# A streaming encoder step on one core: head sums of queries in two one-pass products, and eight attention units behind the gate units of the last projection tile

## The chip, the cores and the metric

The kernel runs on one core of a Trainium2 chip. The metric is the device time of one execution in microseconds. The kernel before takes 1554.57 us, the median of 3 runs (1553.36 to 1554.69). The engines in the profile are PE (TensorE, matrix products), DVE (VectorE), ACT (ScalarE), POOL (GpSimd) and SP (SyncE, which issues most DMAs).

## The reference

The model has two layers with 1024 channels over a prompt of 2048 frames and a sample of 64 frames, all in float32. The second layer is what this change touches:

```
h      = rmsnorm(x1) * norm_b                    # x1: residual stream after layer 1
q | g  = split(h @ w_in_b)                       # 1024 query and 1024 gate channels
q      = per head of 64: q / sqrt(mean(q*q) + eps) * q_norm
p      = softmax over a window of 3 chunks of 64 frames (with a learned sink per head)
y      = (p @ v) * silu(g)
out    = x1 + y @ w_out_b
```

Keys and values (2 heads of 64, each read by 8 query heads) are computed once after layer 1.

## The kernel before

A float32 product that has to be exact enough is made of one-pass products: each operand is split into a high part (rounded, type F32R) and a low part (the rest), and three products high x high, low x high and high x low are summed in PSUM. One row or column of a weight matrix block, 128 output channels by 1024 inputs, is a **unit**: 8 blocks x 3 products = 24 matmuls (line 721). For each unit a weight block is loaded into a slot (line 751, SP), its high part is made by ScalarE (line 770) and its low part by GpSimd (line 775, `low_part`). Slots are reused, and a table says which unit lies in which slot.

The program has four stages: the first projection, the recurrent layer with its output and the keys and values, the second projection (object `b1`), and attention. Each engine runs a program written out by hand, and semaphores (`wait_ge`) tie them together. The numbers in the names say: `t` a tile, `j` the unit in it.

The second projection has 6 tiles of 352 frames (`PT`), with 16 units each: j = 0 to 7 give queries, j = 8 to 15 gates. Units rotate over the four banks `s_banks`; unit j waits until the unit four before it was evacuated. After unit 0 comes the token sum (line 727), which yields the norm of each frame. VectorE evacuates each unit with that norm (line 631). For each query unit ScalarE squares the result (line 513), and TensorE sums the squares per head with one product against `head_ones` in plain float32 (line 705, `head_sum`), in step j + 2. ScalarE takes a square root (line 526), VectorE a reciprocal (line 590) and a product (line 593, `norm_head`). Gates go through silu on ScalarE (line 530). Results are stored to DRAM and attention loads them again. GpSimd makes all low weight parts of the second projection and of the output matrix one after the other, as soon as their slots and high parts are there.

Attention runs in units of 4 heads over 256 frames (the first two units are the sample's, s = 0, then 8 per tile of 256). Per unit: scores (line 1510, in `s_banks`), maximum (1620) and its negation (1624), exponentials (1753), the sum with the sink (1635), its reciprocal (1637), normalisation (1640, 1642), transposes (1525, 1528), values (1555, 1559), product with the gate (1672), high part (1676), low part on GpSimd (1803). From the third unit of s = 2 on, each unit also has one output product of 24 matmuls (line 1573) and an addition (1684). In the loops the transposes of a unit come one unit later and its values two units later. On VectorE `tail_norm` (line 1108) and lines 1101, 1104 belong to the keys of the last recurrent tile, at the start of the second projection; line 1312 (`key_sum`) is their head sum.

## Time and profile before

| | |
|---|---|
| median of 3 runs | 1554.57 us |
| profiled execution | 1552.85 us |
| its span | 1551.0 us |
| busy in the span | PE 96%, DVE 71%, ACT 47%, POOL 16% |
| TensorE's granted clock, mean | 0.989 of full speed |

The span runs from the first to the last instruction of the profiled execution. The second projection lies between about 742 and 1146 us, attention behind it. A busy PE isn't PE at its peak: the columns on the clock say how fast it was allowed to run.

### The profile page before, as it was taken

The numbers are of one execution on the slowest core, as the hardware profiler recorded it, in microseconds if no ns is written. First come the engines' busy times: TensorE is split into PE (matmuls) and PEld (weight loads), VectorE is DVE, ScalarE is ACT, GpSimd is POOL, SyncE is SP. The second block draws the span as 40 slices with busy tenths as digits, with TensorE's granted clock in tenths as the row PEclk, the third lists the DMA queues.
The fourth block names the chain that finished last, engine by engine and source line by source line (L and its number), as shares of the span: only waits on it lengthen the run. The fifth ranks groups of instructions, "written<-read, shape, count | busy, mean of one in ns | idle before, by whom it ended". The sixth has DMA issues, their size and how long they took to land.

```text
span 1551.0 us, 31708 instructions
## 1 busy us (share of the span) xinstructions
PE 1495.9 (96%) x10752; PEld 1427.5 (92%) x10752; DVE 1103.8 (71%) x2244; ACT 734.6 (47%) x1627; POOL 250.0 (16%) x192
## 2 busy tenths in 40 slices
PE   7999999999799999999999999999987999999998
PEld 7999999999799999998899999999975888888888
DVE  7985765758898888897867483755647777777771
ACT  5432322348877777762343342433345444444440
POOL 0000000002444444440530000000321111111110
PEclk9999999999899999999999999999988999999999
DMA  7542432357655555556332121212432444433312
GB/s 244 172 154 90 136 126 102 126 166 226 204 160 157 168 163 157 178 169 206 108 84 68 66 66 56 88 46 89 148 108 71 118 118 115 114 88 95 104 43 81
DMA packets 195500, 193.04 MB, mean 124 GB/s; under 512 B 59696, under 2 KB 188464, under 8 KB 195376
## 3 DMA queue, kind: packets, MB, share of 16 engines
q1 hardware_dynamic: 183248, 182.05, 38.1%
q10 hardware_dynamic: 12128, 9.39, 1.8%
q8 instruction: 71, 1.16, 0.3%
q14 instruction: 53, 0.43, 0.1%
HBM read 119.98 MB, written 71.66 MB: 124 GB/s over the span
## 4 chain that ended last, share of the span: by engine, by line
PE 63%; DVE 4%; ACT 2%; DMA 2%; issue 2%; SPq 0%; ACTq 0%; POOL 0%; DVEq 0%
PE s_banks L721 23%; PE bank L1573 11%; PE bank L1298 10%; PE s_banks L1266 5%; PE s_banks L1510 3%; PE bank L1281 2%; PE bank L1525 2%; PE bank L1555 2%; PE bank L705 2%; PE bank L1559 1%; ACT m_p L1753 1%; DMA x_dram<-r_x 1%; DVE m_nmax L1620 1%; PE bank L1528 1%; DMA sgb_dram<-b_out 1%
## 5 line engine op out<-in xcount | busy, mean ns | idle before, releaser
L1753 ACT ACTIVATE m_p<-s_banks,m_nm 128x192 f32<-128x192 f32 (+2 forms) x264 | 106.3, 415 | 180.8 <-DVE m_nm L1624 180.7
L1573 PE MATMUL bank<-m_y_hi,w_hi_a 128*128 128x256 f32 (+1 forms) x512 | 150.3, 294 | 0.6 <-DVE m_out L1684 0.6
L1573 PE MATMUL bank<-m_y_lo,w_hi_a 128*128 128x256 f32 (+1 forms) x512 | 145.6, 284 | 0.0
L1573 PE MATMUL bank<-m_y_hi,w_lo_a 128*128 128x256 f32 (+1 forms) x512 | 145.5, 284 | 0.0
L721 PE MATMUL s_banks<-b_hi,w_hi_a 128*128 128x352 f32 x384 | 131.3, 342 | 0.0
L721 PE MATMUL s_banks<-b_hi,w_lo_a 128*128 128x352 f32 x384 | 123.9, 323 | 0.0
L721 PE MATMUL s_banks<-b_lo,w_hi_a 128*128 128x352 f32 x384 | 123.8, 322 | 0.0
L590 DVE RECIPROCAL b_qstd<-b_qstd 128x352 f32<-128x352 f32 x48 | 112.6, 2346 | 7.1 <-ACT b_qstd L526 4.8
L721 PE MATMUL s_banks<-b_hi,w_hi_b 128*128 128x352 f32 x336 | 115.7, 344 | 0.0
L721 PE MATMUL bank<-a_hi,w_hi_b 128*128 128x352 f32 x336 | 108.7, 323 | 2.6 <-DVE a_out L631 2.6
L539 ACT ACTIVATE a_out_hi<-a_out 128x352 fp32r<-128x352 f32 (+1 forms) x48 | 23.9, 497 | 183.2 <-DVE a_out L679 183.2
L1298 PE MATMUL bank<-r_y_hi,w_hi_b 128*128 128x264 f32 x384 | 109.1, 284 | 0.6 <-ACT r_std L1203 0.6
L1298 PE MATMUL bank<-r_y_lo,w_hi_b 128*128 128x264 f32 x384 | 108.7, 283 | 0.0
L1298 PE MATMUL bank<-r_y_hi,w_lo_b 128*128 128x264 f32 x384 | 108.7, 283 | 0.0
L721 PE MATMUL bank<-a_hi,w_lo_a 128*128 128x352 f32 x336 | 108.5, 323 | 0.0
L721 PE MATMUL s_banks<-b_hi,w_lo_b 128*128 128x352 f32 x336 | 108.4, 323 | 0.0
L721 PE MATMUL bank<-a_hi,w_hi_a 128*128 128x352 f32 x336 | 108.3, 322 | 0.1
L721 PE MATMUL bank<-a_lo,w_hi_a 128*128 128x352 f32 x336 | 108.4, 323 | 0.0
L721 PE MATMUL s_banks<-b_lo,w_hi_b 128*128 128x352 f32 x336 | 108.3, 322 | 0.0
L721 PE MATMUL bank<-a_hi,w_lo_b 128*128 128x352 f32 x336 | 108.0, 321 | 0.0
L721 PE MATMUL bank<-a_lo,w_hi_b 128*128 128x352 f32 x336 | 107.8, 321 | 0.0
L1241 POOL TENSOR_TENSOR r_ti<-r_ti,r_th 128x528 f32<-128x528 f32 x32 | 42.7, 1334 | 355.6 <-ACT r_th L1164 355.6
(207 smaller groups left out, 4692.8 us busy)
## 6 DMA issues: line engine op xcount, KB each, us to landing
w_raw_a<-weights_dram SPq DMA_DIRECT2D x31, 512.0 KB, 4.9
w_raw_b<-weights_dram SPq DMA_DIRECT2D x20, 512.0 KB, 4.7
sga_dram<-a_out SPq DMA_DIRECT2D x48, 176.0 KB, 1.9
r_xc_hi<-xc_hi_dram SPq DMA_DIRECT2D x32, 264.0 KB, 3.0
r_xc_lo<-xc_lo_dram SPq DMA_DIRECT2D x32, 264.0 KB, 3.3
r_xc<-xc_dram SPq DMA_DIRECT2D x32, 264.0 KB, 3.8
r_sg<-sga_dram SPq DMA_DIRECT2D x32, 264.0 KB, 3.5
r_x<-xT_dram SPq DMA_DIRECT2D x64, 132.0 KB, 2.1
```

What stands on the lines that cost most here:

```text
L590: nc.vector.reciprocal(m.qstd[:, :], m.qstd[:, :]).then_inc(m.qrec_done, 1)
L705: nc.tensor.matmul(bank[5 + q % 2][:, 0:PT], head_ones[:, :], m.q2[:, q % 2, :], start=True, stop=True)\
L721: mm = nc.tensor.matmul(m.banks[j % 4][:, 0:PT], w[pw][:, kt * P:(kt + 1) * P], x[:, kt, :], start=(n == 0), stop=(n == 3 * NB - 1))
L1241: nc.gpsimd.tensor_tensor(r.ti[:, q, :, :], r.ti[:, q, :, :], r.th[:, q, :, :], ALU.mult)\
L1266: mm = nc.tensor.matmul(bank[2 * mat + ob][:, 0:RT], w[pw][:, at:at + P], x[px][:, q, kt, :].bitcast(F32R), start=(i == 0), stop=(i == 5))
L1281: mm = nc.tensor.matmul(bank[6 + o][:, 0:RT], w[pw][:, blk * P:(blk + 1) * P], (r.x1_hi, r.x1_lo)[px][:, blk % 2, :], start=(blk == 0 and ...
L1298: mm = nc.tensor.matmul(bank[4 + blk % 2][:, 0:RT], w[pw][:, kt * P:(kt + 1) * P], (r.y_hi, r.y_lo)[px][tp][:, kt, :], start=(i == 0), sto ...
L1510: mm = nc.tensor.matmul(s_banks[:, 2 * (i % 2) + e, bp * 192 + v0:(bp + 1) * 192], m.q[par][rows, j, blk:blk + 2, :].rearrange("p b t -> p ...
L1525: nc.tensor.transpose(bank[4][:, k * P:(k + 1) * P], m.p[:, i % 2, k, 0:P], ident[:, :])
L1555: nc.tensor.matmul(bank[6][e * HEAD:(e + 1) * HEAD, 0:AT], m.v[par][:, j, n * HEAD:(n + 1) * HEAD], m.pt_a[:, e * AT:(e + 1) * AT], start= ...
L1573: mm = nc.tensor.matmul(out_bank(ts, blk)[:, 0:width], w[pw][:, kt * P:(kt + 1) * P], (m.y_hi, m.y_lo)[px][tp][:, kt, 0:width], start=(n = ...
L1753: nc.scalar.activation(m.p[:, q, k, v0:192], s_banks[:, 2 * q + e, bp * 192 + v0:(bp + 1) * 192], ACT.Exp, bias=m.nm[:, q, k:k + 1], accum ...
```

## The change

**Head sums.** ScalarE makes a high copy of the squares (`q2_hi`), GpSimd subtracts it from the squares (`q2_lo`), and TensorE makes two one-pass products that sum in the bank, in place of one plain float32 product.

**Low weight parts.** GpSimd's list of weight parts no longer runs freely. In the first tile it makes the part of unit j + 2 in step j, ahead of the subtraction of unit j. The parts of the output matrix follow in the last tile's steps from j = 11 on (units 0 to 4), and units 5 to 7 behind attention units s = 1, i = 4 to 6. Slots are dealt out anew for this: the recurrent layer, the first and the second projection and the output matrix use other slots, and two instead of five units of the second projection are loaded behind the last recurrent tile; the unit that was in between is loaded in its tail.

**Gate units.** The eight gate units of the last tile all go to bank 7 (`project_bank`, `late`). Each waits until the unit before was evacuated. Behind each one, `after(s, j)` runs one attention unit on TensorE, VectorE, ScalarE and (two units later) GpSimd: `early_unit` names it, the sample's two units and then the first six of s = 1. The queries of the sample are read from their stores while the gates are still computed. Attention then goes on from unit 8. The gates of the sample have a tensor of their own (`m.sg_sample`). Key scaling and the zeroing of values move to step 6 of the last tile.

The diff, cut to what the prediction speaks of:

```diff
+        def late(m, s, j):
+            return m.heads and isinstance(s, int) and s == PN and j >= NB
+        def project_bank(m, s, j):
+            return bank[7] if late(m, s, j) else m.banks[j % 4]
         def two_pieces(m, s, gate):
...
@@ -512,6 +529,9 @@
                             need(eng, m.qms_done, NB * t + j - 1)
                             nc.scalar.activation(m.q2[:, j % 2, :], m.q[:, j % 4, :], ACT.Square)\
                               .then_inc(m.q2_done, 1)
+                            eng.wait_ge(m.q2_done, NB * t + j + 1)
+                            nc.scalar.activation(m.q2_hi[:, j % 2, :], m.q2[:, j % 2, :], ACT.Copy)\
+                              .then_inc(m.q2_high, 1)
                     blk = input_place(s, j)
                     if blk is not None:
...
@@ -700,9 +720,12 @@
         def project_tensor(eng, m, after):
             def head_sum(t, q):
-                eng.wait_ge(m.q2_done, NB * t + q + 1)
+                eng.wait_ge(m.q2_low, NB * t + q + 1)
                 need(eng, m.qstd_done, NB * t + q - 1)
-                nc.tensor.matmul(bank[5 + q % 2][:, 0:PT], head_ones[:, :], m.q2[:, q % 2, :], start=True, stop=True)\
+                nc.tensor.matmul(bank[5 + q % 2][:, 0:PT], head_ones[:, :].bitcast(F32R), m.q2_hi[:, q % 2, :],
+                                 start=True, stop=False)
+                nc.tensor.matmul(bank[5 + q % 2][:, 0:PT], head_ones[:, :].bitcast(F32R), m.q2_lo[:, q % 2, :],
+                                 start=False, stop=True)\
                   .then_inc(m.qms_done, 1)
             def body(s, par):
...
+                    need(eng, m.evacuated, 2 * NB * t + j - (0 if late(m, s, j) and j > NB else 3))
                     w = slot_of(m.unit + j)
                     for n, (kt, (pw, px)) in enumerate((kt, q) for kt in range(NB) for q in three):
                         if j == 0 and n % 3 == 0:
                             eng.wait_ge(m.x_lo, NB * t + kt + 1)
                         x = (m.hi, m.lo)[px][tp]
-                        mm = nc.tensor.matmul(m.banks[j % 4][:, 0:PT], w[pw][:, kt * P:(kt + 1) * P], x[:, kt, :],
+                        mm = nc.tensor.matmul(project_bank(m, s, j)[:, 0:PT], w[pw][:, kt * P:(kt + 1) * P], x[:, kt, :],
                                               start=(n == 0), stop=(n == 3 * NB - 1))
                     mm.then_inc(m.proj_done, 1)
-                    after(s, j)
                     if m.heads and 2 <= j < NB + 2:
                         head_sum(t, j - 2)
+                    after(s, j)
             run_project(eng, m, body)
```

```diff
+        SLOTS_IN_B = [12, 8, 9, 10, 11, 13, 14, 15] + list(range(8))
         def slot_of(u):
             if u < U_GATE:
                 return slot(SLOTS_IN_A[u - U_A1], a1.extra)
             if u < U_B1:
-                return slot(u - U_GATE)
-            return slot(SLOTS_IN_B[u - U_B1], b1.extra) if u < U_OUT_B else slot(SLOTS_OUT_B[u - U_OUT_B])
+                return slot(SLOTS_IN_R[u - U_GATE])
+            return slot(SLOTS_IN_B[u - U_B1], b1.extra) if u < U_OUT_B else slot(u - U_OUT_B)
...
-            k = last_use[j]
             if m.heads:
-                return U_OUT_B + SLOTS_OUT_B.index(k) if k in SLOTS_OUT_B else None
-            return U_GATE + k if k < UNITS_GATE + UNITS_KV + UNITS_OUT_A else None
+                return U_OUT_B + j - NB if NB <= j < 2 * NB else None
+            return U_GATE + j - 1 if 2 <= j < 2 * NB - 1 else None
+        def project_gpsimd(eng, m, after):
+            def body(s, par):
+                t = s - 1
+                for j in range(2 * NB):
+                    if isinstance(s, int) and s == 1 and j + 2 < 2 * NB:
+                        low_part(eng, nc.gpsimd, m.unit + j + 2)
+                    if j < NB:
+                        eng.wait_ge(m.q2_high, NB * t + j + 1)
+                        nc.gpsimd.tensor_tensor(m.q2_lo[:, j % 2, :], m.q2[:, j % 2, :],
+                                                m.q2_hi[:, j % 2, :].bitcast(F32), ALU.subtract).then_inc(m.q2_low, 1)
+                    after(s, j)
+                    if isinstance(s, int) and s == PN and next_unit(m, j - 3) is not None:
+                        low_part(eng, nc.gpsimd, next_unit(m, j - 3))
+            body(1, 1)
+            with eng.Fori(0, (PN - 2) // 2) as i:
+                body(i * 2 + 2, 0)
+                body(i * 2 + 3, 1)
+            body(PN, PN % 2)
         def recurrent_units(s, g):
```

```diff
+        EARLY_UNITS = 8
+        def early_unit(j):
+            return (0, j - NB) if j < NB + 2 else (1, j - NB - 2)
...
+                    output(ob[0], par if i < 2 else 1 - par, ob[1], AT)
+                if i == 0:
+                    transpose_v(s, par)
+            def after_queries(s, j):
+                if isinstance(s, int) and (s, j) == (1, 0):
+                    key_sum(eng, RN - 1, True)
+                if isinstance(s, int) and s == PN and j >= NB:
+                    es, ei = early_unit(j)
+                    unit(es, es % 2, ei)
...
                     nc.vector.memset(m.vt[1][:, 0:WINDOW], 0.0).then_inc(m.v_zero, 1)
                     scale_keys(0, 0)
+                if isinstance(s, int) and s == PN and j >= NB:
+                    es, ei = early_unit(j)
+                    unit(es, es % 2, ei)
...
+                    high_part(eng, U_OUT_B + i)
+            def after_queries(s, j):
+                if isinstance(s, int) and s == PN and j >= NB:
+                    es, ei = early_unit(j)
+                    unit(es, es % 2, ei)
+            project_scalar(eng, b1, after_queries)
...
-            for i in range(2):
-                nc.gpsimd.memset(m.v_last[i][:, :, :, :], 0.0).then_inc(m.v_last_zero, 1)
-            run_attention(eng, lambda s, par: [low(s, par, i) for i in range(units(s))])
+            def after_queries(s, j):
+                if isinstance(s, int) and (s, j) == (PN, NB - 1):
+                    eng.wait_ge(b1.proj_done, 2 * NB * (PN - 1) + NB)
+                    for i in range(2):
+                        nc.gpsimd.memset(m.v_last[i][:, :, :, :], 0.0).then_inc(m.v_last_zero, 1)
+                if isinstance(s, int) and s == PN and j >= NB + 2:
+                    es, ei = early_unit(j - 2)
+                    low(es, es % 2, ei)
+            def unit(s, par, i):
+                low(s, par, i)
+                if isinstance(s, int) and (s, i) in ((1, 4), (1, 5), (1, 6)):
+                    low_part(eng, nc.gpsimd, U_OUT_B + i + 1)
```

The order of the three engines that pass work between them in the last tile. First ScalarE, behind its last head squares, in the kernel before (`b1_qstd` root of a head sum, `b1_out` silu of a gate, `w_hi_a` high weight part, `m_p` exponentials):

```order
L526 ACTIVATE b1_qstd<-bank5,eps 128x352 [waits b1_q_normed,b1_qms_done]
L530 ACT_TABLE_LOAD
L530 ACTIVATE b1_out<-b1_out 128x352 [waits b1_evacuated]
L770 ACTIVATE w_hi_a<-w_raw_a 128x1024 [waits raw_loaded3]
L526 ACT_TABLE_LOAD [waits b1_q_normed]
L526 ACTIVATE b1_qstd<-bank6,eps 128x352 [waits b1_qms_done]
L530 ACT_TABLE_LOAD
L530 ACTIVATE b1_out<-b1_out 128x352 [waits b1_evacuated] x5
L770 ACTIVATE w_hi_a<-w_raw_a 128x1024 [waits raw_loaded4]
L530 ACTIVATE b1_out<-b1_out 128x352 [waits b1_evacuated]
L770 ACTIVATE w_hi_a<-w_raw_a 128x1024 [waits raw_loaded5]
L530 ACTIVATE b1_out<-b1_out 128x352 [waits b1_evacuated]
```

and after the change:

```order
L546 ACTIVATE b1_qstd<-bank5,eps 128x352 [waits b1_q_normed,b1_qms_done]
L550 ACT_TABLE_LOAD
L550 ACTIVATE b1_out<-b1_out 128x352 [waits b1_evacuated]
L1827 ACT_TABLE_LOAD
L1827 ACTIVATE m_p,m_den<-s_banks,m_nm 128x192 [waits m_nm_done]
L1827 ACTIVATE m_p,m_den<-s_banks,m_nm 128x192 x3
L1832 ACTIVATE m_es<-m_sm 128x4 [waits m_sm_done]
L1844 ACTIVATE m_v0<-bank4 128x128 [waits m_vt_done]
L546 ACT_TABLE_LOAD [waits b1_q_normed]
L546 ACTIVATE b1_qstd<-bank6,eps 128x352 [waits b1_qms_done]
L550 ACT_TABLE_LOAD
L550 ACTIVATE b1_out<-b1_out 128x352 [waits b1_evacuated]
```

A load of ScalarE's function table now stands on both sides of each silu, because exponentials follow it.

VectorE at the same place, before (`b1_out<-s_banks` evacuates a gate unit):

```order
L631 TENSOR_TENSOR b1_out<-s_banks,b1_std 128x352 [waits b1_stored2]
L590 RECIPROCAL b1_qstd<-b1_qstd 128x352 [waits b1_qstd_done,b1_proj_done,b1_rstd_done]
L593 TENSOR_TENSOR b1_out<-b1_q,b1_qstd 128x352 [waits b1_stored0,b1_qrec_done]
L631 TENSOR_TENSOR b1_out<-s_banks,b1_std 128x352 [waits b1_stored3]
L590 RECIPROCAL b1_qstd<-b1_qstd 128x352 [waits b1_qstd_done,b1_proj_done,b1_rstd_done]
L593 TENSOR_TENSOR b1_out<-b1_q,b1_qstd 128x352 [waits b1_stored1,b1_qrec_done]
L631 TENSOR_TENSOR b1_out<-s_banks,b1_std 128x352 [waits b1_stored2]
L631 TENSOR_TENSOR b1_out<-s_banks,b1_std 128x352 [waits b1_stored3,b1_proj_done,b1_rstd_done]
```

and after (the sums and normalisations of an attention unit, on `m_p`, are what follows each evacuation):

```order
L613 TENSOR_TENSOR b1_out<-b1_q,b1_qstd 128x352 [waits b1_stored1,b1_qrec_done]
L651 TENSOR_TENSOR b1_out<-bank7,b1_std 128x352 [waits b1_stored2]
L1691 TENSOR_REDUCE m_nmax<-s_banks 128x4 [waits m_s_done]
L1695 TENSOR_TENSOR m_nm<-m_nmax,neg_sink 128x4 [waits m_max_done]
L1699 TENSOR_TENSOR m_sm<-m_nm,sink 128x4 [waits m_nm_done]
L1706 TENSOR_TENSOR m_dsum<-m_den,m_es 128x4 [waits m_es_done,m_exp_done]
L1708 RECIPROCAL m_rden<-m_dsum 128x4 [waits m_dsum_done]
L1711 TENSOR_TENSOR m_p_last<-m_p,m_rden 128x256 [waits m_rden_done]
L1713 TENSOR_TENSOR m_p<-m_p,m_rden 128x4x128
L1728 COPY m_v_last0<-bank5 64x128 [waits m_v_last_zero,m_vt_done]
L1730 COPY m_v_last0<-bank5 64x128
L1680 TENSOR_SCALAR m_k1<-m_k1,kq_scale 128x2x256 [waits m_tile_loaded1]
```

Between two evacuations VectorE now has the maximum, the sums and the products of one attention unit, which wait for ScalarE's exponentials.

GpSimd from the last recurrent tile's low parts on, before:

```order
L775 TENSOR_TENSOR w_lo_b<-w_raw_b,w_hi_b 128x1024 [waits w_high] x4
L775 TENSOR_TENSOR w_lo_a<-w_raw_a,w_hi_a 128x1024 [waits w_high] x2
L775 TENSOR_TENSOR w_lo_b<-w_raw_b,w_hi_b 128x1024 [waits w_high] x2
L775 TENSOR_TENSOR b1_w_lo<-b1_w_raw,b1_w_hi 128x1024 [waits w_high]
L775 TENSOR_TENSOR w_lo_a<-w_raw_a,w_hi_a 128x1024 [waits w_high] x8
L1808 MEMSET m_v_last0 128x1024 [waits b1_evacuated]
L1808 MEMSET m_v_last1 128x1024
L1803 TENSOR_TENSOR m_y_lo0<-m_y,m_y_hi0 128x4x64 [waits m_y_high] x2
L1803 TENSOR_TENSOR m_y_lo1<-m_y,m_y_hi1 128x4x64 [waits m_y_high] x8
```

and after, from the last tile of the second projection on (`x8` counts equal rows):

```order
L862 TENSOR_TENSOR b1_q2_lo<-b1_q2,b1_q2_hi 128x352 [waits b1_q2_high] x8
L1891 MEMSET m_v_last0 128x1024 [waits b1_proj_done]
L1891 MEMSET m_v_last1 128x1024
L1884 TENSOR_TENSOR m_y_lo0<-m_y,m_y_hi0 128x4x64 [waits m_y_high] x2
L799 TENSOR_TENSOR w_lo_a<-w_raw_a,w_hi_a 128x1024 [waits w_high]
L1884 TENSOR_TENSOR m_y_lo1<-m_y,m_y_hi1 128x4x64 [waits m_y_high]
L799 TENSOR_TENSOR w_lo_a<-w_raw_a,w_hi_a 128x1024 [waits w_high]
```

GpSimd had all weight parts done ahead of the first attention unit; now they alternate with the low parts of attention's results, up to unit 8 of attention.

## Rows read from the trace of the kernel before

**Rows 1.** Chain that ended last, share of the span by engine.

```profile
PE 63%; DVE 4%; ACT 2%; DMA 2%; issue 2%; SPq 0%; ACTq 0%; POOL 0%; DVEq 0%
```

**Rows 2.** Chain in order of time, 738 to 775: start us, us, what.

```profile
748.75 0.71 PE bank L1312 x2
...
757.15 0.70 PE bank L705 x2
...
761.68 0.59 PE bank L705 x2
```

**Rows 3.** Chain in order of time, 1100 to 1240.

```profile
1113.48 3.82 PE s_banks L721 x24
...
1206.92 2.83 PE bank L1573 x24
...
1212.43 2.83 PE bank L1573 x24
```

**Rows 4.** Timeline of VectorE, ScalarE, TensorE: start us, us, instruction, [idle before].

```profile
1020.87 0.96 DVE L631 TENSOR_TENSOR b_q<-s_banks,b_std 128x352 f32<-128x352 f32 x2 [0.22 <-DVE b_std L613]
...
1021.50 0.89 ACT L513 ACTIVATE b_q<-b_q 128x352 f32<-128x352 f32 x2 [3.24 <-DVE b_q L631]
...
1023.83 0.75 PE L705 MATMUL bank<-b_q,head_ones 128*128 128x352 f32 x2
...
1032.90 0.53 DVE L631 TENSOR_TENSOR b_q<-s_banks,b_std 128x352 f32<-128x352 f32 x1 [0.24 <-PE s_banks L721]
```

**Rows 5.** Groups by line: busy us, mean ns of one, idle before.

```profile
L590 DVE RECIPROCAL b_qstd<-b_qstd 128x352 f32<-128x352 f32 x48 | 112.6, 2346 | 7.1 <-ACT b_qstd L526 4.8
...
L1803 POOL TENSOR_TENSOR m_y_lo<-m_y,m_y_hi 128x256 fp32r<-128x256 f32 x66 | 48.7, 737 | 316.7 <-DVE m_y_hi L1676 316.7
...
L1241 POOL TENSOR_TENSOR r_ti<-r_ti,r_th 128x528 f32<-128x528 f32 x32 | 42.7, 1334 | 355.6 <-ACT r_th L1164 355.6
```

**Rows 6.** Timeline of GpSimd and VectorE, 741 to 760.

```profile
743.36 12.47 POOL L775 TENSOR_TENSOR w_lo_a<-w_raw_a,w_hi_a 128x1024 fp32r<-128x1024 f32 x5 [37.25 <-DVE b_lo L403]
...
746.27 2.43 DVE L1104 TENSOR_TENSOR r_k<-r_k 128x264 f32<-128x264 f32 x1
...
751.91 1.66 DVE L1110 SCALAR_TENSOR_TENSOR r_k<-r_k,vec,r_std 128x264 f32<-128x264 f32 x1
...
755.87 0.96 DVE L631 TENSOR_TENSOR b_q<-s_banks,b_std 128x352 f32<-128x352 f32 x2
```

**Rows 7.** Timeline of ScalarE, gate units of the last tile.

```profile
1121.00 0.56 ACT L526 ACTIVATE b_qstd<-bank,eps 128x352 f32<-128x352 f32 x1 [2.95 <-DVE b_out L593]
1121.57 1.28 ACT L530 ACT_TABLE_LOAD   x1
1122.87 0.50 ACT L530 ACTIVATE b_out<-b_out 128x352 f32<-128x352 f32 x1
1123.27 1.04 ACT L770 ACTIVATE w_hi_a<-w_raw_a 128x1024 fp32r<-128x1024 f32 x1
```

**Rows 8.** Timeline of VectorE and GpSimd there.

```profile
1118.12 2.40 POOL L775 TENSOR_TENSOR w_lo_a<-w_raw_a,w_hi_a 128x1024 fp32r<-128x1024 f32 x1 [2.05 <-ACT w_hi_a L770]
...
1119.79 1.12 DVE L593 TENSOR_TENSOR b_out<-b_q,b_qstd 128x352 f32<-128x352 f32 x1
...
1124.22 0.53 DVE L593 TENSOR_TENSOR b_out<-b_q,b_qstd 128x352 f32<-128x352 f32 x1
```

**Rows 9.** Timeline of VectorE in attention, units 8, 11 and 12.

```profile
1186.69 0.95 DVE L1620 TENSOR_REDUCE m_nmax<-s_banks 128x4 f32<-128x768 f32 x1
...
1201.45 0.96 DVE L1620 TENSOR_REDUCE m_nmax<-s_banks 128x4 f32<-128x768 f32 x1
...
1204.55 0.16 DVE L1635 TENSOR_TENSOR m_dsum<-m_den,m_es 128x4 f32<-128x4 f32 x1 [0.72 <-ACT m_es L1758]
...
1205.91 0.95 DVE L1620 TENSOR_REDUCE m_nmax<-s_banks 128x4 f32<-128x768 f32 x1
```

**Rows 10.** Busy time by stretch: PE, PEld, DVE, ACT, POOL, then clock, DMA.

```profile
1154.00:1158.00 4.00, 2.57 (x14) 2.08 (x14) 2.56 (x9) 2.21 (x10) 0.00 (x0) 0.53 0.30 102
```

221 lines of the change are left out of this document (119 added, 102 removed).

## The prediction

> **What bounds the kernel now.** I read the chain of waits first. By its summary [rows 1] TensorE carries 63% of the span, most of it the projection matmuls of line 721, so an edit counts when it shortens TensorE's work or opens a hole in it. The chain in order of time [rows 2] shows the second projection: a unit of 24 matmuls, then the head sum of line 705 (two rows in the trace), and so on without a hole. One such step is 761.68 + 0.59 - 757.85 = 4.42 us, 3.83 of it the unit, so 0.16 a matmul. In the last tile and in attention [rows 3] this changes. The first gate unit ends at 1113.48 + 3.82 = 1117.30, and behind the last of them VectorE and ScalarE pass each unit between them, until at 1206.92 the output matmuls (2.83 us per unit) come in and TensorE is the bound again. I call 1117.30 zero: before, the maximum of attention unit 8 starts at 69.4 and that of unit 12 at 88.6 [rows 9]. What the change does to this second number passes to the end one for one, since everything behind it is TensorE's.
>
> **Head sums.** There are 8 in each of 6 tiles, 48. Each takes 0.59 and would take two matmuls of a unit's kind, 0.32. Gain 0.27; the last two are in the gate part below, so 46 x 0.27 = **-12.4**. Bounds: 0 each if the new pair runs no faster than the old, 0.43 if one of the two hid entirely. The price of a one-pass product with these widths is in the trace thousands of times, so I take 0.27.
> The new copy on ScalarE costs about 0.4 to 0.5 (its square of the same size is 0.89 for two) and GpSimd's subtraction lies between 0.74 for 256 columns and 1.33 for 528, by length 0.95 [rows 4, 5]. Where is it late? At the first head sum of a tile: both evacuations come at 1020.87, the first square starts at 1021.50, the second is in front of nothing, so ready at 1021.5 + 0.45 + 0.5 + 0.95 + hops = 1023.6, and TensorE asks at 1023.83. Slack 0.2; with 1.33 it is late by 0.2, six times 1.2 us at most. Cost 0. The next pacer is VectorE: of the old step of 4.43 it idles 0.24 [rows 4], so it needs 4.19 and the new step is 4.16. It falls behind by a few hundredths per query unit, which four banks and the gate units absorb.
>
> **Start of the second projection.** Before, GpSimd makes five weight parts back to back from 743.36, and two VectorE products that have both inputs in SBUF take 2.43 and 1.66 us, beside 0.4 to 0.5 for their like [rows 6]. After, GpSimd makes one part and then waits for a head square. So the key sum of 748.75 is 0.95 earlier (it then follows unit 0), and the first evacuation, 755.87 now, comes near 753.35 (0.95, and 1.2 from the product at 751.91, and 0.4 of hops). But the low part of unit 3 now stands behind the first square's subtraction: 753.35 + 0.5 + 0.6 + 0.5 gives 755.0, subtraction to 755.95, weight part of 2.4 to 758.4. Unit 3 starts at 758.45 where it started at 757.85, and the head sum ahead of it, 0.70 there, had its gain booked above: **+1.0**. Bounds 0 (if it is ready) and 3.5 (if each later part is as late too; GpSimd needs 3.35 per unit, TensorE 4.16, so it catches up). Moved weight loads (three fewer behind the last recurrent tile, one more inside its tail) I price at 0, of -2 to +2: they lie beside TensorE work that waits for none of them in rows 2.
>
> **Gate units with attention behind them.** All eight gate units of the last tile now use one bank, so each waits until VectorE has evacuated the last, and VectorE does one attention unit in between. That makes a ring: evacuation, silu, high weight part, table load, exponentials, normalisation, next evacuation. Prices: table load 1.28, silu 0.4, high part 0.95 to 1.04 [rows 7]; VectorE's maximum to the sum of denominators 3.10, of it 1.95 behind the maximum and its negation, which is the exponentials' time, and that sum to the next maximum 1.36 [rows 9].
> Unit 0: head norm of 2.35 + 0.53 [rows 5, 8] and evacuation to 3.4; the square root of head 6 on ScalarE to 3.55, load, silu, load, to 6.65; exponentials 1.6, normalisation and the copies of v and keys, to 11.0. Unit 1: norm to 13.8, evacuation 14.2; ScalarE's load for the last square root waits for that norm: three loads, square root and silu to 18.7, exponentials and normalisation to 22.05. Unit 2: norm and evacuation to 25.3, silu, high part, load to 28.1, the short exponentials and the copy behind them to 30.0. TensorE's transposes wait for that copy and gate unit 11 is queued behind them: 31.1 to 35.0. TensorE has by then stood some 7 us.
> Such holes cost clock. In 1154 to 1158, where TensorE waits for the other engines between attention units, the granted clock was 0.53 [rows 10], near the lower of the two levels (1.2 of 2.4 GHz); 4 us at that cost 1.9 of full speed. I take 2 for unit 11, so 37.0. Unit 3's normalisation ends at 43.4. Then the ring turns at 0.4 + 0.95 + 1.28 + 1.95 + 1.4 + 0.5 + hops of 0.2 = 6.7, plus 0.4 to 0.6 of the next effect: 50.3, 57.3, 64.6, 72.0 for units 4 to 7. TensorE needs 3.84 plus the small products, which are 1212.43 - 1206.92 - 2.83 = 2.68 [rows 3], so 6.5, and is not the ring's bound. Unit 8's maximum is at 72.0: **+2.6**.
> The next effect: a VectorE operation with two SBUF inputs that meets GpSimd's subtraction waits for its end. Line 593 took 1.12 while GpSimd's part of 1118.12 ran, and 0.53 without [rows 8]. The low weight parts of the output units now stand in GpSimd's order between the low parts of attention, one per step from gate unit 11 on, and three more behind units 6, 7 and 8, that is during units 8, 9 and 10. Such a part begins some 0.8 after the high y of its step and runs 2.4; the sum of denominators (line 1635, two SBUF inputs) then waits for its end. In units 8 to 10 it would start 3.1 after the maximum does; GpSimd's part starts some 2.8 after it and ends at 5.2, so it starts 2.1 later: 3 x 2.1 = 6.3. Before, no part was left there. With the 2.6, and 0.1 of hops, unit 12's maximum is at 97.6 instead of 88.6: **+9.0**. Bounds: 0 (no lock; then the 0.4 to 0.6 of each ring turn goes too) and 16 (every part holds VectorE 2.4 us).
> By the Trainium skill (SBUF — State Buffer, Who interferes with whom) a VectorE instruction with two SBUF inputs and a GpSimd instruction that reads SBUF take turns on a shared port pair, the later one fully blocked. Line 593's 1.12 agrees, and without the rule the sum would be that of the first rival.
>
> **The sum.** -12.4 + 1.0 + 9.0 = -2.4 on a span of 1551.0: 1548.6. The profiled execution took 1552.85, 1.85 above its span and 1.72 under the median 1554.57 of the runs. From the median: **1552.2 us**. Within 0.2%, 3.1 us, a measurement can't tell it from no change.
>
> **Rivals.**
> No lock in the attention steps: GpSimd's part starts after VectorE's small operations, or gives way. The region is then +1.0, not +9.0: 1554.57 - 12.4 + 1.0 + 1.0 = 1544.2. For it: line 1635 takes 0.16 and touches 4 columns. Against: line 1104 and line 593.
> The ring doesn't bind: TensorE stays full, steps of 6.5. Unit 8's maximum is then at 52.4 and the sum -12.4 + 1.0 - 17.0 + 6.3 = -22.1: 1532.5. Against: table loads have to come off the ring, and three head norms of 2.9 stand in it.
> Slower, by the clock: after the holes of some 5 and 7 us TensorE stays at the lower level for further gate units. Each takes 3.84 more and the small products with it; its step becomes 7.7 + 2.7 = 10.4 instead of 7.1, +3.3. One such unit gives 1555.5 (no change); two 1558.8, three 1562.1. It decides from two units on. For it: 0.53 over 1154 to 1158, where TensorE was busy 2.57 of 4 us [rows 10]. Against: there TensorE worked in shreds, a gate unit is 24 matmuls without a hole.
> Slower, by the table: eleven table loads stand on the ring (two at unit 0, three at unit 1, one each at 2 to 7), and a change of table could cost more than its row, since ScalarE's pipe has to run empty ahead of it. If that costs the row's 1.28 once more, the ring is 11 x 1.28 = 14.1 longer: 1566.3. Against: the silu starts 0.02 after the load's end, and the load 0.01 after the square root of 0.56 at 1121.00 [rows 7].
> The Trainium skill (ScalarE: Activation LUTs, What ACT_TABLE_LOAD costs) gives a drain of some 1.38 us beside each load of 1.283. The trace shows the 1.28 and no such drain at 1121.57; by the page the time would be about 1567.
> That the change doesn't do what it says would show as head sums still at 0.59: 1564.6. No chance worth a number; the same kind of product stands next to it.
>
> **Chances.** Forecast 0.42, its own range 1549 to 1556 (0.5 each side on the lock per step, 1.2 late head sums, 2 for the loads). No lock 0.20. Full TensorE 0.08. Clock 0.20 (one unit 0.07, more 0.13). Table 0.05. Anything else 0.05. The range 1543 to 1562 leaves out the full TensorE, the table, and half of the last: 0.16. Faster, under 1551.5: 0.16 of the forecast's 0.42, the 0.20, the 0.08 and 0.02, so 0.46. Slower, over 1557.7: 0.13 + 0.05 + 0.02 + 0.01 = 0.21. Same: 0.33.
>
> **What would show it.** Step of a query unit in the second projection 4.16 instead of 4.43; the pair at 0.32. Unit 3's start near 758.5. From the end of the first gate unit: evacuations at about 3, 14, 25, 37, then every 7.1 to 7.3; unit 8's maximum at 72; the sum of denominators of units 8 to 10 starting as a GpSimd weight part ends; unit 12's maximum at 97.6. Granted clock near 0.5 only around gate unit 11. The prediction is wrong if the ring turns in less than 6.6 or more than 8, if line 1635's counterpart does not wait for GpSimd, or if TensorE has holes at the head sums of the first five tiles.

## The result and the profile after

| | before | after |
|---|---|---|
| median | 1553.96 us (4 runs, 1553.09 to 1554.69) | 1571.76 us (4 runs, 1568.28 to 1576.02) |
| profiled execution | 1552.85, span 1551.0 | 1570.4, span 1568.6 |
| mean granted clock | 0.989 | 0.981 |

The ratio is 1.0115, 95% interval 1.0102 to 1.0127: the change makes the kernel slower by 1.15%, clear of the scatter, and by 17.6 us of span, where 2.4 us faster was forecast. It lies above the forecast range.

Two words are used below. The **lock** is the effect that the prediction called the next effect: a VectorE operation with two SBUF inputs that meets a running GpSimd subtraction waits for its end. A **ring** is a set of engines that wait for each other in turn, so that each step starts only when the last one has gone round.

Where it went, by the places at which both kernels can be cut. The cuts are the starts of the token sums of the tiles (line 727 before, 752 after), the end of the last tile's first gate unit and the start of the first output matmul (the last two by the chain of waits).

| stretch | before | after | difference | forecast |
|---|---|---|---|---|
| start to token sum of tile 1 | 747.15 | 749.19 | +2.0 | 0 |
| to token sum of tile 2 | 68.45 | 83.46 | **+15.0** | -1.2 |
| to token sum of tile 6 | 266.75 | 258.78 | -8.0 | -8.6 |
| to end of first gate unit | 34.95 | 33.49 | -1.5 | -1.6 |
| to first output matmul | 89.6 | 102.6 | **+13.0** | +9.0 |
| to the end | 344.1 | 341.1 | -3.0 | 0 |

The timeline of TensorE before, then after, has the cuts of the first tile:

```profile
747.15 0.75 PE L727 MATMUL bank<-b_acc,ones 128*128 128x352 f32 x2
...
815.60 0.75 PE L727 MATMUL bank<-b_acc,ones 128*128 128x352 f32 x2
```

```profile
749.19 0.75 PE L752 MATMUL bank<-b_acc,ones 128*128 128x352 f32 x2
...
832.65 0.75 PE L752 MATMUL bank<-b_acc,ones 128*128 128x352 f32 x2
...
897.81 0.75 PE L752 MATMUL bank<-b_acc,ones 128*128 128x352 f32 x2
```

The summary of the chain of waits after answers to [rows 1], and its order of time in a later tile to [rows 2]. The head sum is now a pair of 0.16, and a query step 4.14 (1043.62 less 1039.48):

```profile
PE 56%; DVE 7%; issue 5%; ACT 3%; DMA 2%; POOL 1%; SPq 0%; ACTq 0%; DVEq 0%; POOLq 0%
```

```profile
1039.48 0.16 PE bank L725
1039.64 0.17 PE bank L727
1039.80 3.81 PE s_banks L746 x24
1043.62 0.16 PE bank L725
```

**The first tile.** The timelines of VectorE and of GpSimd for one query step of tile 1, after:

```profile
778.10 0.51 DVE L651 TENSOR_TENSOR b_q<-s_banks,b_std 128x352 f32<-128x352 f32 x1
778.53 2.34 DVE L610 RECIPROCAL b_qstd<-b_qstd 128x352 f32<-128x352 f32 x1
780.90 2.60 DVE L613 TENSOR_TENSOR b_out<-b_q,b_qstd 128x352 f32<-128x352 f32 x1
783.43 0.57 DVE L412 SCALAR_TENSOR_TENSOR b_lo<-b_x,vec,b_hi 128x352 fp32r<-128x352 f32 x1
...
784.36 0.51 DVE L651 TENSOR_TENSOR b_q<-s_banks,b_std 128x352 f32<-128x352 f32 x1
```

```profile
779.83 0.94 POOL L862 TENSOR_TENSOR b_q_lo<-b_q,b_q_hi 128x352 fp32r<-128x352 f32 x1 [2.97 <-ACT b_q_hi L533]
780.73 2.39 POOL L799 TENSOR_TENSOR w_lo_a<-w_raw_a,w_hi_a 128x1024 fp32r<-128x1024 f32 x1
```

The evacuation at 778.10 releases the square, its copy, GpSimd's subtraction at 779.83 and, right behind it, a weight part from 780.73 to 783.12. VectorE's product of line 613 (0.53 alone) is due at 780.90 and ends 0.38 behind that part. The next evacuation is 6.26 behind the last, and so the next subtraction: a ring that puts the part on the product again. The eight products of line 613 in this tile take 0.74, 2.53, 2.60, 2.60, 2.60, 0.52, 2.58 and 0.53, and three other operations with two SBUF inputs (lines 412 and 425) take 2.70 to 2.72. TensorE, with 4.16 of work a step, is no longer the bound. Its waits from 742 to 833 show whom it waits for (total, times, longest):

```profile
PE bank L725 <- ACT b_qstd L546: 5.7, 4, 1.9
PE s_banks L746 <- DVE b_out L651: 5.4, 2, 3.4
```

The root of line 546 stands behind VectorE's product, so 11.1 us are waits for a late VectorE; the longest, 3.4, has a late store on the way (VectorE idles 2.42 for it). For GpSimd itself TensorE waits 1.9: 1.7 for the weight part of unit 3, which starts 12.1 behind the token sum (10.7 before, 11.3 forecast), and 0.2 for a subtraction.

**From the gate units on.** VectorE's evacuations, with the idle time ahead of them, in the timeline after (line 651), its maximum of units 8 and 12 (line 1691) and the sum of denominators of unit 8 (1706), and GpSimd's weight part there. They answer to [rows 8, 9]:

```profile
1127.83 0.52 DVE L651 TENSOR_TENSOR b_out<-bank,b_std 128x352 f32<-128x352 f32 x1
...
1138.86 0.52 DVE L651 TENSOR_TENSOR b_out<-bank,b_std 128x352 f32<-128x352 f32 x1
...
1154.33 0.53 DVE L651 TENSOR_TENSOR b_out<-bank,b_std 128x352 f32<-128x352 f32 x1 [4.16 <-DMA sgb_dram<-b_out]
...
1168.03 0.53 DVE L651 TENSOR_TENSOR b_out<-bank,b_std 128x352 f32<-128x352 f32 x1 [4.41 <-issue]
...
1201.67 0.95 DVE L1691 TENSOR_REDUCE m_nmax<-s_banks 128x4 f32<-128x768 f32 x1
...
1204.77 2.08 DVE L1706 TENSOR_TENSOR m_dsum<-m_den,m_es 128x4 f32<-128x4 f32 x1 [0.32 <-ACT m_es L1832]
...
1226.51 0.95 DVE L1691 TENSOR_REDUCE m_nmax<-s_banks 128x4 f32<-128x768 f32 x1
```

```profile
1204.48 2.36 POOL L799 TENSOR_TENSOR w_lo_a<-w_raw_a,w_hi_a 128x1024 fp32r<-128x1024 f32 x1
```

With 1124.92, the end of the first gate unit, as zero the evacuations come at 2.9, 13.9, 29.4 and 43.1 (forecast 3, 14, 25, 37), the maximum of unit 8 at 76.8 (forecast 72.0, before 69.4) and that of unit 12 at 101.6 (forecast 97.6, before 88.6). The third evacuation waited for a store. The timeline of SyncE's queue says why: it stood for 43 us over the eight stores of query heads, the last of which waits for a product of VectorE at 1149.65, and the first gate's store is behind them, with the first output weight's load behind that:

```profile
1107.52 43.01 SPq L476 DMA_DIRECT2D qn_dram<-b_out  x8
1150.58 0.43 SPq L1461 DMA_DIRECT2D m_sg_sample<-sgb_dram  x1
1151.05 0.68 SPq L476 DMA_DIRECT2D sgb_dram<-b_out  x1
1151.84 0.37 SPq L776 DMA_DIRECT2D w_raw_a<-weights_dram  x1
```

ScalarE then waits for that load, TensorE for both (busy time by stretch, columns as in [rows 10]; third number of the waits row is the longest):

```profile
1157.02 1.06 ACT L794 ACTIVATE w_hi_a<-w_raw_a 128x1024 fp32r<-128x1024 f32 x1 [1.63 <-DMA w_raw_a<-weights_dram]
```

```profile
1130.00:1134.00 4.00, 4.00 (x16) 4.00 (x15) 0.34 (x2) 3.63 (x12) 0.00 (x0) 0.50 0.00 0
...
1152.00:1158.00 6.00, 0.00 (x0) 0.00 (x0) 2.58 (x8) 1.48 (x2) 0.73 (x1) 0.50 1.01 294
1158.00:1164.00 6.00, 2.68 (x11) 2.65 (x12) 2.08 (x6) 4.32 (x14) 0.00 (x0) 0.50 0.77 275
1164.00:1170.00 6.00, 6.00 (x46) 5.40 (x45) 1.85 (x6) 3.07 (x4) 0.00 (x0) 0.88 0.01 4
```

```profile
PE bank L1603 <- ACT m_pt_a L1838: 14.9, 2, 13.0
```

The first of the stretches is gate unit 9: it too ran at the lower clock level, behind a wait of TensorE of 2.6 us. It cost nothing here, since VectorE had work until 1136.05 and the unit ended at 1135.9; its evacuation comes at 13.9 or 14.0 in every kernel with this order and the silu, also where the unit ended 2.8 us earlier. From gate unit 12 to 15 TensorE has no wait at all, with steps of 6.3 to 6.5 us, and VectorE's ring turns in 6.6 to 6.85. The granted clock is again 0.50 at 1202 to 1206 and 1214 to 1222, in attention units 8 to 10; no run separates what that costs.

### The profile page after: what moved, and what is told of

Same layout as the page of the kernel before. It is cut to its first block, busy times and chain, and to the rows that moved or that the text cites. A ratio compares the mean times of both kernels' runs of the same rounds, so it can differ in the third digit from the quotient of the medians.

```text
span 1568.6 us, 31868 instructions
## 1 busy us (share of the span) xinstructions
PE 1487.5 (95%) x10752; PEld 1427.8 (91%) x10752; DVE 1118.0 (71%) x2244; ACT 775.1 (49%) x1688; POOL 295.2 (19%) x240
## 4 chain that ended last, share of the span: by engine, by line
PE 56%; DVE 7%; issue 5%; ACT 3%; DMA 2%; POOL 1%; SPq 0%; ACTq 0%; DVEq 0%; POOLq 0%
PE s_banks L746 17%; PE bank L1637 11%; PE bank L1347 10%; PE s_banks L1315 5%; PE s_banks L1569 3%; PE bank L1330 2%; PE bank L1584 2%; PE bank L1619 2%; ACT m_p L1827 1%; PE bank L1623 1%; DVE b_qstd L610 1%; DMA x_dram<-r_x 1%; PE bank L1587 1%; PE bank L746 1%; DVE m_dsum L1706 1%
## 5 line engine op out<-in xcount | busy, mean ns | idle before, releaser
L746 PE MATMUL bank<-a_hi,w_lo_a 128*128 128x352 f32 x384 | 124.0, 323 | 0.0
L1884 POOL TENSOR_TENSOR m_y_lo<-m_y,m_y_hi 128x256 fp32r<-128x256 f32 x66 | 48.7, 738 | 342.3 <-DVE m_y_hi L1748 342.3
L1347 PE MATMUL bank<-r_y_hi,w_hi_a 128*128 128x264 f32 x384 | 109.3, 285 | 0.6 <-ACT r_std L1245 0.6
L746 PE MATMUL s_banks<-b_hi,w_hi_a 128*128 128x352 f32 x320 | 104.2, 326 | 5.4 <-DVE b_out L651 5.4
L1347 PE MATMUL bank<-r_y_lo,w_hi_a 128*128 128x264 f32 x384 | 109.1, 284 | 0.0
L1347 PE MATMUL bank<-r_y_hi,w_lo_a 128*128 128x264 f32 x384 | 108.8, 283 | 0.0
L746 PE MATMUL s_banks<-b_hi,w_lo_a 128*128 128x352 f32 x320 | 104.3, 326 | 0.0
L746 PE MATMUL s_banks<-b_lo,w_hi_a 128*128 128x352 f32 x320 | 104.2, 326 | 0.0
L862 POOL TENSOR_TENSOR b_q_lo<-b_q,b_q_hi 128x352 fp32r<-128x352 f32 x48 | 45.4, 948 | 287.5 <-ACT b_q_hi L533 287.5
L1637 PEld LDWEIGHTS bank<-m_y_hi,w_hi_a 128*128 128x128 f32 x512 | 96.5, 188 | 0.9 <-issue 0.9
```

Source lines behind the costliest of these rows:

```text
L746: mm = nc.tensor.matmul(project_bank(m, s, j)[:, 0:PT], w[pw][:, kt * P:(kt + 1) * P], x[:, kt, :], start=(n == 0), stop=(n == 3 * NB - 1))
L862: nc.gpsimd.tensor_tensor(m.q2_lo[:, j % 2, :], m.q2[:, j % 2, :], m.q2_hi[:, j % 2, :].bitcast(F32), ALU.subtract).then_inc(m.q2_low, 1)
L1347: mm = nc.tensor.matmul(bank[4 + blk % 2][:, 0:RT], w[pw][:, kt * P:(kt + 1) * P], (r.y_hi, r.y_lo)[px][tp][:, kt, :], start=(i == 0), sto ...
L1637: mm = nc.tensor.matmul(out_bank(ts, blk)[:, 0:width], w[pw][:, kt * P:(kt + 1) * P], (m.y_hi, m.y_lo)[px][tp][:, kt, 0:width], start=(n = ...
L1884: nc.gpsimd.tensor_tensor(y_part(m.y_lo, s, par, i), m.y[:, q, :, :], y_part(m.y_hi, s, par, i).bitcast(F32), ALU.subtract).then_inc(m.y_l ...
```

## The experiments

All ratios are against the kernel before, on the same chip. "T1" is token sum to token sum of the first tile (83.5 after, 68.5 before). "R" is first gate unit's end to first output matmul; where the head sums of the last tile are those of the changed kernel, that end is taken as the last token sum plus 33.5. R is read here from the timeline, where the output matmul starts 0.24 earlier than in the chain of the table: 102.4 after, 89.4 before. In experiments 1, 2 and 4, which leave the gate units as they are, R is 101.7, 102.0 and 101.7, so differences of R under 0.7 say nothing.

**1. No weight parts in the first tile.** In `project_gpsimd` a GpSimd memset, which reads nothing and takes 0.9, stands in the place of the subtraction; the kernel leaves out the low weight parts of units 2 to 15.

```diff
+        def low_mark(eng, ops, u):
...
+            ops.memset(low.bitcast(F32), 0.0)\
...
-                        low_part(eng, nc.gpsimd, m.unit + j + 2)
+                        low_mark(eng, nc.gpsimd, m.unit + j + 2)
```

> Left out: GpSimd's subtraction for the low weight parts of units 2 to 15 of the second projection; a GpSimd memset of the same tile, which reads nothing, stands in its place (0.9 us), so every wait, load and high part is kept. Measured so far: from the token sum of the first tile to that of the second 83.5 us in the changed kernel, 68.5 before, 64.5 to 65.2 in the other tiles of the changed kernel. Lock theory (VectorE's products with two SBUF inputs wait for the running weight part, which stands behind the square's subtraction and so meets them in every step): this distance falls to 65 to 66, the span by 17 to 18, to about 1551. Rival, late weight loads or high parts: they are all still there, so the distance stays above 80. Rival, ScalarE's added copies: also unchanged.

Measured, as expected: T1 66.0, span 1551.9, ratio 1.001 (1.000 to 1.0021), 1553.93 us. The 17.4 us of tile 1 are the running parts'; loads, high parts and copies, all still there, have no share. By itself this doesn't say whether the parts cost by the lock or by GpSimd's time; TensorE's waits above and the two experiments that follow do.

**2. Plain head sums in the first tile.**

```diff
+                            if not (isinstance(s, int) and s == 1):
+                                eng.wait_ge(m.q2_done, NB * t + j + 1)
+                                nc.scalar.activation(m.q2_hi[:, j % 2, :], m.q2[:, j % 2, :], ACT.Copy)\
...
+                if isinstance(t, int) and t == 0:
...
+                    nc.tensor.matmul(bank[5 + q % 2][:, 0:PT], head_ones[:, :], m.q2[:, q % 2, :], start=True, stop=True)\
```

> The changed kernel with plain float32 head sums in the first tile alone (no copy, no subtraction there), so GpSimd's weight parts of that tile run as soon as their high parts are there; tiles 2 to 6 keep the two products. Lock theory in the form 'it is the order behind the subtraction that puts the part on VectorE's products': token sum to token sum of the first tile 68 to 70 instead of 83.5 (before: 68.5), span 1553 to 1556. Rival, the new slots and weight loads of this tile are late whatever GpSimd does: still over 80, span within 2 us of 1568.6. Rival, it is the mere number of parts and not their place: over 75, since the parts are the same.

Measured: T1 71.3, a little over what was expected, span 1555.0, ratio 1.0037 (1.0023 to 1.0051), 1556.84 us. Both rivals fall. The same fourteen parts, no longer behind a subtraction, cost nothing like 15: the eight products of line 613's counterpart took 0.53, 0.59, 0.64, 0.98, 0.79, 1.29, 2.60 and 0.53, and TensorE waits for none of them. Not the number of parts matters, but when they run: seven of them run one behind the other from 744.27 to 761.4, ahead of the first of these products (766.88), and most of the others lie for the most part beside a reciprocal. The 2.9 over 68.45 come from another place (9 below).

**3. The head-sum part alone, in all tiles**, on the kernel before: no gate part, no new slots or loads.

> The kernel before with the head-sum part of the change in all six tiles and nothing of the gate part, the slots or the loads: in the first tile GpSimd alternates weight part j + 2 and the subtraction of square j, as in the changed kernel; in the last tile it makes the eight subtractions and then the output weight parts. If the 15 us of the first tile come from this alternation alone, token sum to token sum of the first tile is 80 to 84 here too, the other tiles 64.5, attention as before: 1551.0 + 13.5 - 10.5 = 1554 span, ratio 1.001 to 1.003. Rival, the new slots and loads had a share in it: first tile under 76, ratio under 0.998.

Measured: T1 83.6, the other tiles 64.6, ratio 1.0033 (1.0022 to 1.0044), 1557.82 us. The loss of the first tile belongs to the alternation on GpSimd alone, without the new slots and loads. R is 91.7, 2.3 over before, though attention is untouched; 9 below shows the same.

**4. The same work in another place.** Each weight part waits for an evacuation and runs ahead of the subtraction:

```diff
+                        if j + 3 < 2 * NB:
+                            eng.wait_ge(m.evacuated, j + 1)
+                            low_part(eng, nc.gpsimd, m.unit + j + 3)
```

> The changed kernel with the same work on GpSimd in the first tile in another place: each weight part waits for the evacuation of a query unit and runs ahead of the square's subtraction, so 2.4 us of it lie beside VectorE's reciprocal of 2.35, which reads one SBUF tile. Place theory (not the amount of GpSimd's work costs, but that it meets two-input products): only the subtraction meets line 613's product, steps of 4.9 to 5.0 in place of 6.25, and none blocked from unit 8 on: token sum to token sum of the first tile 69 to 72 instead of 83.5, span 1554 to 1557. Amount theory (GpSimd's 3.35 us a step and VectorE's 1.4 of two-input work can't share 4.16): over 78 whatever the order.

Measured: T1 79.1, span 1563.2, 1566.16 us, ratio 1.0091 (1.0076 to 1.0107). The expectation of 69 to 72 failed, and the number lies where amount theory had it, over 78. The steps say which theory holds where. Three query steps in a row did what place theory said: 4.92 each, for 6.26. The timeline of VectorE, then GpSimd, in that kernel:

```profile
774.29 2.33 DVE L610 RECIPROCAL b_qstd<-b_qstd 128x352 f32<-128x352 f32 x1
776.66 0.57 DVE L613 TENSOR_TENSOR b_out<-b_q,b_qstd 128x352 f32<-128x352 f32 x1
777.16 1.26 DVE L412 SCALAR_TENSOR_TENSOR b_lo<-b_x,vec,b_hi 128x352 fp32r<-128x352 f32 x1
```

```profile
774.45 2.40 POOL L799 TENSOR_TENSOR w_lo_a<-w_raw_a,w_hi_a 128x1024 fp32r<-128x1024 f32 x1 [1.33 <-DVE b_q L651]
776.82 1.22 POOL L866 TENSOR_TENSOR b_q_lo<-b_q,b_q_hi 128x352 fp32r<-128x352 f32 x1
```

The part lies beside the reciprocal and blocks nothing; the subtraction waits for line 613 (1.22 in place of 0.94) and then holds line 412. But 4.92 is still more than TensorE's 4.16, and from unit 8 on each part now waits for a VectorE that is late, and TensorE waits for the parts, 8.7 us in three waits:

```profile
PE s_banks L746 <- POOL w_lo_a L799: 8.7, 3, 4.7
```

So the place of a part decides what it costs VectorE, and amount theory isn't refuted as a whole: no order that was tried fits a subtraction and a part into each step of 4.16.

**5. No output weight parts** (a memset in their place; the kernel leaves out the low parts of the output matrix).

> Left out: GpSimd's subtraction for the low weight parts of the eight output units; a memset that reads nothing in its place. Measured: from the end of the last tile's first gate unit to the first output matmul 102.6 us after the change, 89.6 before. Lock theory: the sums of denominators of attention units 8, 9 and 10, which take 2.08 us each, fall to 0.16 (-5.8), and those of the steps before lose 0.25 to 0.65 each (-1.5): 95 to 96 us. Rival, they wait for ScalarE's exponentials and not for GpSimd: over 101.

Measured: R 96.8 (first output 1218.0, first gate unit's end 1121.2), 0.8 over the expectation, span 1561.3, 1565.14 us, ratio 1.0094 (1.0072 to 1.0116). The sum of denominators of unit 8 is the row below, 0.16 in place of 2.08, as the lock theory has it. The ring of gate units 12 to 15 turns in 6.3 to 6.6, which is TensorE's own step:

```profile
1199.73 0.16 DVE L1712 TENSOR_TENSOR m_dsum<-m_den,m_es 128x4 f32<-128x4 f32 x1 [0.73 <-ACT m_es L1838]
```

**6. The order of five stores**: the first gate's ahead of head 6, the second's ahead of head 7.

```diff
+                        out_j = (8, 6, 9, 7, 10)[out_j]
```

> The changed kernel with another order of five stores on SyncE in the last tile: the first gate unit ahead of query head 6, the second ahead of head 7. Queue theory: in the changed kernel SyncE stands at the store of head 7 until 1150.58, so the first gate's store and the first output weight's load are issued only then; gate unit 10's evacuation waits for that store (idle 4.16) and the high part for the load. With the new order the evacuation of gate unit 10 comes about 25.5 us after the end of gate unit 8 instead of 29.4, the high part follows at once, and the distance from gate unit 8 to the first output matmul is 102.6 - 4.1 - 1.6 = 96.9, perhaps 2 more off for a shorter TensorE hole. Rival, the evacuation was going to wait for TensorE or the clock anyway: over 101.

Measured: R 96.8, evacuation of gate unit 10 at 25.1, 1564.61 us, ratio 1.0084 (1.0067 to 1.0101). R and evacuation are as expected. In the profile of this run T1 is 80.8 and the tile behind it 69.9 (65.2 in the changed kernel), where TensorE waits 3.4 for the first subtraction; why is open, and only R is read from it. The wait at gate unit 11 stayed (5.00 of idle time):

```profile
1163.28 0.53 DVE L656 TENSOR_TENSOR b_out<-bank,b_std 128x352 f32<-128x352 f32 x1 [5.00 <-issue]
```

**7. A copy in place of silu** in the last tile; the kernel leaves out the silu of these gates, and its result is another one for it.

```diff
-                            nc.scalar.activation(m.out[:, place(m, j), 0:PT], m.out[:, place(m, j), 0:PT], ACT.Silu)\
+                            nc.scalar.activation(m.out[:, place(m, j), 0:PT], m.out[:, place(m, j), 0:PT],
+                                                 ACT.Copy if late(m, s, j) else ACT.Silu)\
```

> Left out: the silu of the last tile's eight gate units, a plain copy of the same size stands in its place; so the exponential's table stays loaded and ten of the table loads of 1.28 us between the gate units are gone (the one for the last square root and the one behind it stay). Table as priced (1.28 each, no drain): the ring of units 0 and 1 loses 1.28 each, units 2 and 3 1.28 each, units 4 to 7 0.1 to 0.3 each, since TensorE's 6.5 and GpSimd's weight part bound them at once: from the first gate unit's end to the first output matmul 96.5 to 98 instead of 102.6. Rival, each load costs its row and a drain of about as much again: units 0 to 3 lose 2.6 each, below 93. Rival, the loads lie beside other waits: over 101.

Measured: R 98.7, 0.7 over what was expected and between the two rivals (below 93, over 101), 1566.38 us, ratio 1.0086 (1.007 to 1.0101). From unit 0's maximum to its sum of denominators it took 3.91 in place of 5.33, with one load less, and in unit 1 5.19 in place of 6.62: 1.42 a load, the row's 1.28 and the gaps around it. No drain. In gate units 12 to 15 the loads were gone and the ring turned as before, 6.6 and 6.85: the sum of denominators, due 1.4 earlier (3.58 behind the evacuation, not 5.01), now waited for GpSimd's part (row below), and TensorE, with steps of 6.3 to 6.5 and no wait there, left no more than 0.3 a turn to be won in any case:

```profile
1173.56 1.83 DVE L1707 TENSOR_TENSOR m_dsum<-m_den,m_es 128x4 f32<-128x4 f32 x1 [1.04 <-ACT m_es L1833]
```

**8. Three mends together** (2, 6, and the last three output parts held by the diff below until a later unit's negated maximum), then **8b** with one more: TensorE's transposes of values behind gate unit 11 instead of ahead of it.

```diff
+                    eng.wait_ge(m.nm_done, unit_of(s, i) + 4)
```

> Three mends of the changed kernel together: plain head sums in the first tile, the store order of the last run, and the last three output weight parts held until the negated maximum of a later unit is there, so that they run beside the exponentials. First tile 71.3 (as run with the first mend alone); first gate unit to first output 96.8 with the second; of the 5.8 us in units 8 to 10 the third takes about 3 (the part then ends 0.4 after the sum of denominators is due, and the low y behind it costs another 0.6): 93.5 to 94.5. Sum: 1551.0 + 2.9 - 8.2 - 1.5 + 4.5 = 1548.7 span, 0.2% under before, ratio 0.998. If the third gives nothing: 1551.5.

> The three mends together (first gate unit to first output 94.6, ratio 0.998), and TensorE's transposes of the values of attention unit 2 moved behind gate unit 11. They wait for ScalarE's copy of the probabilities, and gate unit 11 was queued behind them: a hole of 7.0 us on TensorE, then a gate unit at the lower clock (5.0 us of VectorE's waiting). Now gate unit 11 follows gate unit 10's evacuation at once. If hole and clock are what the ring lost there: 4 to 5 us less, first gate unit to first output 90 to 91, ratio 0.995. Rival, the hole moves behind gate unit 11 and the clock falls for the small products and unit 12 instead: under 1.5 us, ratio 0.9975.

Measured: 8 has R 94.6, 1549.59 us, ratio 0.998 (0.997 to 0.999). 8b has R 91.7, 1546.3 us, ratio 0.9954 (0.9941 to 0.9968); there gate unit 11's evacuation is 7.6 behind that of unit 10, where it was 11.3 in 8, so most of the hole and its clock were real, though R fell by 2.9 and not by 4. The rival, under 1.5, falls. Both are faster than before, 8b by as much as two of the three kernels with head sums alone that follow:

**9. Head sums alone, where GpSimd is free.** On the kernel before: **9a** in tiles 2 to 5, **9b** in tile 6 too, **9c** as 9b and with this diff at the start:

```diff
-            low_units(eng, U_B1 + 2, U_OUT_B)
+            low_units(eng, U_B1 + 2, U_B1 + 3)
+            eng.wait_ge(r.k2_done, RN)
+            low_units(eng, U_B1 + 3, U_OUT_B)
```

> The kernel before with one part of the change, and only where GpSimd has nothing else to do: head sums in two one-pass products in tiles 2 to 5 of the second projection (copy on ScalarE, subtraction on GpSimd); tiles 1 and 6, the gate units, the slots and loads are those of before. My theory: 32 head sums x 0.27 = 8.6 off, tiles of 64.5 to 64.7 instead of 66.6 to 66.8, ratio 0.9945. Rival, VectorE paces the query units at 4.2 or the subtraction comes late: tiles above 66. Rival, the gain is given back in attention: tiles of 64.6 but a ratio over 0.998.

> As the run with head sums in two products in tiles 2 to 5 (ratio 0.995), and in tile 6 too: there GpSimd makes the eight subtractions first and the output weight parts behind them, beside the gate units, where VectorE waits for stores. 8 x 0.27 = 2.2 more off: ratio 0.9935. Rival, the late output parts meet VectorE at the start of attention, or the first output matmuls wait for them: ratio 0.995 to 0.998.

> As the last, and at the start of the second projection GpSimd makes the part of unit 2 only and then waits for VectorE's product of the last keys (2.43 us beside a running part, 0.42 alone) before it goes on. The key sum then follows unit 0 at once: the hole of TensorE there, 0.8 in the profile of before and 2.4 in two later ones, goes, and with it the stretch of lower clock behind it (0.66 over 750 to 755 in those two): 1.5 to 3.5 less than the last kernel, ratio 0.992. Rival, the next part meets the product behind the key sum instead (1.66 at line 1110) and holds the first evacuation: no gain, 0.9935.

Measured: 9a 1545.18 us, 0.995 (0.9936 to 0.9964); 9b 1546.41 us, 0.9959 (0.9945 to 0.9972); 9c **1542.85 us**, 0.9937 (0.9923 to 0.995), the fastest kernel of the study. The intervals of the three overlap. 9a is the gain that was forecast per head sum. 9b gained nothing: token sum of tile 6 to first output is 125.1 against 122.4 in 9a (124.3 before, with the same code there as 9a). Its trace shows the wait. Its first six output parts now run one behind the other for 15.03 from 1109.04 on, and three of the last four head products take 2.58, 1.84 and 1.84 (first row: the first of them in 9b; in 9a they take 0.65, 1.12 and 0.52). So the last query stores are late and SyncE stands 21.58 over five of them (second row) where it stands 18.05 in 9a (third row); the gate stores behind them, and the evacuations that wait for those, come late. It is the lock and the order of stores once more:

```profile
1109.23 2.58 DVE L601 TENSOR_TENSOR b_out<-b_q,b_qstd 128x352 f32<-128x352 f32 x1
...
1105.57 21.58 SPq L471 DMA_DIRECT2D qn_dram<-b_out  x5
...
1106.39 18.05 SPq L471 DMA_DIRECT2D qn_dram<-b_out  x5
```

9c against 9b is the key product at the start. In 9a, as in 2 and 8, TensorE waited for it (first row: the waits of 9a) and ran at a clock of 0.66 over 750 to 755 (second row: 9a by stretch; third: 9c, clock 1.00):

```profile
PE bank L1329 <- DVE r_k L1121: 2.4, 1, 2.4
```

```profile
750.00:755.00 5.00, 5.00 (x21) 4.93 (x22) 3.77 (x3) 1.87 (x3) 5.00 (x3) 0.66 0.47 153
```

```profile
750.00:755.00 5.00, 4.92 (x32) 4.63 (x30) 4.78 (x5) 0.59 (x2) 5.00 (x3) 1.00 0.44 137
```

T1 is 71.5 in 9a and 9b and 68.3 in 9c: these are the 3 us that experiment 2 had left. The tile behind it gives 0.6 of them back (66.2 for 65.6), where TensorE waits 1.4 for the first subtraction, 0.7 in 9b.

## Why the prediction was wrong

**The step that failed: the start of the second projection, "+1.0".** It said that GpSimd needs 3.35 per unit and TensorE 4.16, "so it catches up", and gave 3.5 as the upper bound. That treats GpSimd as a queue with a rate. What it does to VectorE, which the same text used for attention (rows 8) and even for the first microseconds of this stage (rows 6), was not asked of the steps behind them. The alternation of subtraction and weight part hangs on each evacuation and so puts the part on the two-input product: 2.5 to 2.6 for 0.53 in five of eight products, steps of 6.26 for 4.16. Experiments 1, 2 and 3 show it from three sides. The stretch came out 16.2 over its forecast (+15.0 for -1.2), four fifths of the whole miss of 20.0. No rival that was named has this mechanism; the one by the tables (1566.3) lies nearest in number, and experiment 7 refutes it, so that nearness is chance. One of the prediction's signs of being wrong, holes at the head sums of the first five tiles, did show: four in the first tile.

**The second step, "Gate units with attention behind them", +9.0, measured +13.0.** Its lock was right: 2.08 each in units 8 to 10 (forecast 2.1), and the ring's last leg 24.8 for 25.6. The ring turned in 6.6 to 6.85, not 7.1 to 7.3; the part delayed the sum of denominators by some 0.25 and not 0.5, which is part of it. What was missed is SyncE: every wait of a moved store was to be listed, and the order of stores across query heads and gates was not. It costs 4.3 at gate unit 10 and 1.6 for the load behind it; experiment 6 gave 5.6 back. What the lower clock cost at gate unit 11 was 2, as taken: 6.7 from the transposes at 1161.32 to the evacuation, where they and the unit need 4.6 at the upper level.

**Right:** 0.27 for each head sum outside the first tile (tiles 3 to 5 take 64.5 to 64.65 where 64.4 to 64.6 follows; tile 2, with a wait of 0.2, 65.2), no hole at the first head sum of tiles 3 to 6, table loads at their row's price. The rival by a drain is refuted (1.42 a load, not 2.66), as is the one without a lock. The one by the clock is refuted in what it costs, not in what it says: gate unit 9 ran at the lower level as well as 11, while VectorE was the later of the two. (That rival's sum also left the small products at 2.7, though it slowed them.) Full TensorE fails in the first four steps, where TensorE waits up to 13.0; in gate units 12 to 15 it is full, and only 0.3 a step faster than the ring.

**The start, +2.0, booked at 0 with bounds of -2 to 2.** The first token sum starts at 744.8 to 747.2 in the five profiles with the old slots and loads and at 746.0 to 749.8 in the nine with the new ones, 1.7 later on average. So a share of it may well be the moved loads'; it is not shown. In the changed kernel VectorE idles 1.27 for a load of the residual in the last recurrent tile, 0.58 before, and TensorE waits 4.6 for line 1118 from 690 on, 3.5 before; no experiment takes the loads back.

**Not shown to be the change's:** the end, -3.0. From the first output matmul the twelve profiles of the experiments need 341.5 to 346.1. An output unit of 24 matmuls takes 2.83 throughout in the profile before, and 2.74 for about half of them in that of the changed kernel (a matmul 281 or 276 ns), which makes some 2.6 of the 3.0. Both levels occur within one kernel. What sets them stays open.
